# The first norm of a two-block kernel: x in four loads, the bias transposes moved behind the first units, and one matmul for the second half's sum

## The reference, cut to what matters

```python
def rmsnorm(x, g):
    xf = x.astype(jnp.float32)
    y = xf * lax.rsqrt(jnp.mean(xf * xf, axis=-1, keepdims=True) + EPS)
    return (y * g.astype(jnp.float32)).astype(x.dtype)

# first_block
h = rmsnorm(x, norm_mix[l])
proj = h @ w_in[l]
zu, zv, zq, zf, zi, zo, g_a, g_b = jnp.split(proj, split_points, axis=-1)
...
# second_block: the only use of the bias b_ada
mod = (c_act @ w_ada[l] + b_ada[l]).reshape(b, N_MOD, 1, D_MODEL)
```

## Time and profile before

| what | us |
|---|---|
| median of 3 runs | 2746.13 (2746.02 to 2748.16) |
| the profiled execution | 2748.0 |
| its span in the profile | 2745.8 |
| mean granted TensorE clock | 0.997 |
| PE busy | 2710.0 |
| DVE busy | 1425.8 |
| ACT busy | 926.3 |
| POOL busy | 69.2 |

### The profile page before, as it was taken

The page is one execution under the profiler, slowest core; times in us unless marked ns, Lnnn a source line. Parts: engine busy times, 40 slices in busy tenths (PEclk is TensorE's granted clock), DMA queues, the critical chain, the costliest instruction groups (busy, mean ns, idle before and its releaser), DMA issues.

```text
span 2745.8 us, 32619 instructions
## 1 busy us (share of the span) xinstructions
PE 2710.0 (99%) x13015; PEld 2264.0 (82%) x13015; DVE 1425.8 (52%) x1590; ACT 926.3 (34%) x1153; POOL 69.2 (3%) x119
## 2 busy tenths in 40 slices
PE   8999999999999999999989999999999999999999
PEld 7888988888888788888768888888888888888887
DVE  6677563586667675657445323353333454533333
ACT  4555442332223322224444222243222332432221
POOL 1000000000000000001200000000000000000000
PEclk9999999999999999999999999999999999999999
DMA  4111223555664455654112332223323323233322
GB/s 140 58 63 63 69 87 105 179 199 197 208 210 162 156 198 198 218 189 127 47 46 92 103 97 92 89 94 101 99 92 98 101 84 101 85 99 101 98 92 77
DMA packets 257851, 323.67 MB, mean 118 GB/s; under 512 B 5734, under 2 KB 248676, under 8 KB 249572
## 3 DMA queue, kind: packets, MB, share of 16 engines
q1 hardware_dynamic: 245872, 245.12, 28.0%
q0 software_dynamic: 9216, 75.50, 7.4%
q10 hardware_dynamic: 2676, 1.84, 0.2%
HBM read 320.34 MB, written 2.10 MB: 117 GB/s over the span
## 4 chain that ended last, share of the span: by engine, by line
PE 96%; DVE 2%; ACT 1%; issue 0%; DMA 0%; DVEq 0%; ACTq 0%
PE po L682 25%; PE po L683 25%; PE po L684 25%; PE pm L905 2%; PE po L867 1%; PE po L869 1%; PE po L868 1%; PE po L747 1%; PE po L749 1%; PE po L762 1%; PE po L782 1%; PE po L787 1%; PE po L777 1%; PE po L859 1%; PE po L861 1%; PE po L860 1%
## 5 line engine op out<-in xcount | busy, mean ns | idle before, releaser
L1925 DVE TENSOR_TENSOR w_lo<-w_raw,w_hi 128x1024 fp32r<-128x1024 f32 x472 | 562.7, 1222 | 448.3 <-ACT w_hi L1334 445.9
L1334 ACT ACTIVATE w_hi<-w_raw 128x1024 fp32r<-128x1024 f32 x470 | 477.1, 1051 | 886.9 <-PE po L684 869.2
L682 PE MATMUL po<-a_hi,w_hi 128*128 128x512 f32 x1856 | 722.8, 389 | 0.0
L684 PE MATMUL po<-a_hi,w_lo 128*128 128x512 f32 x1856 | 722.1, 389 | 0.0
L683 PE MATMUL po<-a_lo,w_hi 128*128 128x512 f32 x1856 | 722.0, 389 | 0.0
L684 PEld LDWEIGHTS po<-a_hi,w_lo 128*128 128x128 f32 x1856 | 348.3, 188 | 72.8
L682 PEld LDWEIGHTS po<-a_hi,w_hi 128*128 128x128 f32 x1856 | 348.4, 188 | 72.6 <-issue 0.2
L683 PEld LDWEIGHTS po<-a_lo,w_hi 128*128 128x128 f32 x1856 | 348.4, 188 | 71.9 <-issue 0.2
L682 PE MATMUL po<-b_hi,w_hi 128*128 128x512 f32 x1024 | 399.0, 390 | 0.0
L684 PE MATMUL po<-b_hi,w_lo 128*128 128x512 f32 x1024 | 398.4, 389 | 0.0
L683 PE MATMUL po<-b_lo,w_hi 128*128 128x512 f32 x1024 | 398.3, 389 | 0.0
(11 more groups left out here) (380 smaller groups left out, 2862.5 us busy)
## 6 DMA issues: line engine op xcount, KB each, us to landing
ada_in<-in_w_ada_dram POOLq DMA_DIRECT2D x64, 1152.0 KB, 5.5
w_raw<-in_ffn_wg_dram SPq DMA_DIRECT2D x44, 1024.0 KB, 5.3
w_raw<-in_ffn_wu_dram SPq DMA_DIRECT2D x44, 1024.0 KB, 5.3
w_raw<-in_w_ff_dram SPq DMA_DIRECT2D x32, 1024.0 KB, 5.4
w_raw<-in_ffn_wd_dram SPq DMA_DIRECT2D x32, 1024.0 KB, 5.0
w_raw<-in_w_in_dram SPq DMA_DIRECT2D x27, 1024.0 KB, 5.1
w_raw<-in_ffn_wd_dram SPq DMA_DIRECT2D x16, 768.0 KB, 4.3
w_raw<-in_w_in_c_dram SPq DMA_DIRECT2D x12, 1024.0 KB, 5.1
```

What stands on the lines that cost most here:

```text
L682: pe.matmul(o, wh, hi[:, k, :], start=(k == ks[0]), stop=False)
L684: mm = pe.matmul(o, wl, hi[:, k, :], start=False, stop=(k == ks[-1]))
L1334: act.activation(w_hi[:, s, part], w_raw[:, s, part], ACT.Copy).then_inc(hi_done, 1)
L1925: dve.tensor_tensor(w_lo[:, s, part], w_raw[:, s, part], w_hi[:, s, part].bitcast(F32), ALU.subtract).then_inc(lo_done, 1)
```

## The change

Four things are done.

- x comes in four loads of 128 tokens each, with a semaphore each. `turn(j, h, t)` transposes one token block of a quad, two transposes, and PE waits for each load and then transposes its part of all four quads; the quad is announced with the second of its blocks. Quad 3 of half b is now transposed and copied with the others, before the vectors, and DVE's copy of it no longer stands between t1 and t2.
- ACT's square of quad 2 of half b stands before the log of half a, instead of behind its root.
- For half b POOL adds the two sums once more (`quad`), and then the two 256-column halves of the result (`fold`), and PE needs one matmul, `sum_of_second`, instead of four.
- The two bias transposes move on PE from before the first half's sum to behind `first_products`.

```diff
-            for h in range(2):
-                sp.dma_start(x_in[:, 2 * h:2 * h + 2, :],
-                             x[0, 2 * h * P:2 * (h + 1) * P, :].rearrange("(t p) d -> p t d", p=P))\
-                    .then_inc(x_landed[h], 16)
+            for t in range(NT):
+                sp.dma_start(x_in[:, t, :], x[0, t * P:(t + 1) * P, :]).then_inc(x_landed[t], 16)
...
+            pool.wait_ge(s_pre_pool, pre_pool.after("add2b"))
+            pool.tensor_tensor(sq_mix[:, 1, 0, :], sq_mix[:, 1, 0, :], sq_mix[:, 1, 2, :], ALU.add)\
+                .then_inc(s_pre_pool, pre_pool.one("quad"))
+            pool.wait_ge(s_pre_pool, pre_pool.after("quad"))
+            pool.tensor_tensor(sq_mix[:, 1, 0, H[0]], sq_mix[:, 1, 0, H[0]], sq_mix[:, 1, 0, H[1]], ALU.add)\
+                .then_inc(s_pre_pool, pre_pool.one("fold"))
...
-            def turn(j, h):
+            def turn(j, h, t):
                 dst = pm[:, j, :] if h == 0 else po[:, j // 2, j % 2, :]
                 for b in range(2):
-                    for t in range(2):
-                        mm = pe.transpose(dst[:, (2 * b + t) * P:(2 * b + t + 1) * P],
-                                          x_in[:, 2 * h + t, (2 * j + b) * P:(2 * j + b + 1) * P], ident[:, :])
-                mm.then_inc(s_pre_pe, pre_pe.one(f"x{j}{'ab'[h]}"))
+                    mm = pe.transpose(dst[:, (2 * b + t) * P:(2 * b + t + 1) * P],
+                                      x_in[:, 2 * h + t, (2 * j + b) * P:(2 * j + b + 1) * P], ident[:, :])
+                if t:
+                    mm.then_inc(s_pre_pe, pre_pe.one(f"x{j}{'ab'[h]}"))
...
+            def sum_of_second():
+                pe.wait_ge(s_pre_pool, pre_pool.after("fold"))
+                pe.matmul(pm[:, 1, H[1]], ones[:, :], sq_mix[:, 1, 0, H[0]], start=True, stop=True)\
+                    .then_inc(s_n_pe, norm_pe["mix"].one("sumb"))
+
+            for h in range(2):
+                for t in range(2):
+                    pe.wait_ge(x_landed[2 * h + t], 16)
+                    for j in range(QUADS):
+                        turn(j, h, t)
             pe.wait_ge(vec_landed, 12 * 16)
             pe.wait_ge(s_pre_dve, pre_dve.after("x2a"))
             pe.transpose(pm[:, 2, 0:112], vec_rows[0:112, :], ident[0:112, 0:112])\
                 .then_inc(s_pre_pe, pre_pe.one("vec"))
-            turn(QUADS - 1, 1)
-            pe.wait_ge(s_pre_dve, pre_dve.after("x3a"))
-            for l in range(2):
-                if l == 1:
-                    pe.wait_ge(s_pre_dve, pre_dve.after("vec"))
-                pe.transpose(pm[:, 3 - l, 0:MODS], b_rows[:, l, :], ident[0:MODS, 0:MODS])\
-                    .then_inc(s_pre_pe, pre_pe.one(f"b{l}"))
-            first_sum_of(0)
+            sum_of_first()
...
             first_products(U_HG, "mix")
+            for l in range(2):
+                pe.transpose(pm[:, 3 - l, 0:MODS], b_rows[:, l, :], ident[0:MODS, 0:MODS])\
+                    .then_inc(s_pre_pe, pre_pe.one(f"b{l}"))
             product(0, U_HG + 2, DK, a_hi, a_lo)
...
                 first_weight_hi(0)
+                square(2, "b")
                 log("a")
                 root("a")
-                square(2, "b")
                 square(3, "b")
...
                 t(0, "a")
                 t(1, "a")
-                turned(QUADS - 1, "b")
                 t(2, "a")
```

More of the change, by code:

```diff
@@ L244, in hybrid_two_block_kernel @@
         out_taken = [sem("out_taken0"), sem("out_taken1")]
-        x_landed = [sem("x_landed0"), sem("x_landed1")]
+        x_landed = [sem(f"x_landed{t}") for t in range(NT)]
         first_landed = sem("first_landed")
@@ L271, in hybrid_two_block_kernel @@
         s_o_pe, s_o_dve, s_o_act = sem("out_pe"), sem("out_dve"), sem("out_act")
[L274 to L278, removed]
+        pre_pe = Steps(s_pre_pe, [f"x{j}{half}" for half in "ab" for j in range(QUADS)] + ["vec", "b0", "b1"])
+        pre_dve = Steps(s_pre_dve, ["zero"] + [f"x{j}{half}" for half in "ab" for j in range(QUADS)]
+                        + ["vec", "b0", "b1", "c1", "c2", "c3"])
+        pre_pool = Steps(s_pre_pool, ["add0a", "add2a", "add0b", "add2b", "quad", "fold"])
         pre_act = Steps(s_pre_act, ["ec"])
@@ L290, in hybrid_two_block_kernel @@
             if name == "mix":
-                names = ["sq0a", "sq1a", "sq2a", "sq3a", "sq0b", "sq1b", "lna", "rstda", "sq2b", "sq3b"]
+                names = ["sq0a", "sq1a", "sq2a", "sq3a", "sq0b", "sq1b", "sq2b", "lna", "rstda", "sq3b"]
                 names += ["hi0a", "hi1a", "hi2a", "hi3a", "lnb", "hi4a", "rstdb", "hi5a", "hi6a", "hi7a"]
@@ L750, in first_products @@
                         if half == "a" and k == 2 and name == "mix":
-                            first_sum_of(1)
+                            sum_of_second()
                         elif half == "a" and k == 2:
@@ L811, in _, with sum_of_first @@
             pe.wait_ge(consts_ready, 15)
-            def turn(j, h):
+            def turn(j, h, t):
                 dst = pm[:, j, :] if h == 0 else po[:, j // 2, j % 2, :]
                 for b in range(2):
-                    for t in range(2):
-                        mm = pe.transpose(dst[:, (2 * b + t) * P:(2 * b + t + 1) * P],
-                                          x_in[:, 2 * h + t, (2 * j + b) * P:(2 * j + b + 1) * P], ident[:, :])
-                mm.then_inc(s_pre_pe, pre_pe.one(f"x{j}{'ab'[h]}"))
-            def first_sum_of(h):
+                    mm = pe.transpose(dst[:, (2 * b + t) * P:(2 * b + t + 1) * P],
+                                      x_in[:, 2 * h + t, (2 * j + b) * P:(2 * j + b + 1) * P], ident[:, :])
+                if t:
+                    mm.then_inc(s_pre_pe, pre_pe.one(f"x{j}{'ab'[h]}"))
+            def sum_of_first():
                 for j in (0, 2):
-                    pe.wait_ge(s_pre_pool, pre_pool.after(f"add{j}{'ab'[h]}"))
+                    pe.wait_ge(s_pre_pool, pre_pool.after(f"add{j}a"))
                     for b in range(2):
-                        mm = pe.matmul(pm[:, h, H[h]], ones[:, :], sq_mix[:, h, j, H[b]],
+                        mm = pe.matmul(pm[:, 0, H[0]], ones[:, :], sq_mix[:, 0, j, H[b]],
                                        start=(j == 0 and b == 0), stop=(j == 2 and b == 1))
[L827 to L834, removed]
+                mm.then_inc(s_n_pe, norm_pe["mix"].one("suma"))
+            def sum_of_second():
[7 more added lines that the diff above has]
+                        turn(j, h, t)
             pe.wait_ge(vec_landed, 12 * 16)
@@ L2071, in t @@
                                              ALU.mult, ALU.mult).then_inc(nd.sem, nd.one(f"t{k}{half}"))
[L2073 to L2076, removed]
+                for half in "ab":
+                    for j in range(QUADS):
+                        turned(j, half)
                 dve.wait_ge(s_pre_pe, pre_pe.after("vec"))
@@ L2088, in first_norm @@
                 for k in range(4, DK):
-                    if k == DK - 2:
-                        dve.wait_ge(s_pre_dve, pre_dve.after(f"x{QUADS - 1}b"))
                     t(k, "a")
```

## The result

| | before | changed kernel |
|---|---|---|
| median, us | 2746.23 (13 runs) | 2754.05 (13 runs) |
| lowest to highest | 2746.02 to 2748.45 | 2751.34 to 2754.87 |
| span of the profiled execution | 2745.8 | 2751.9 |

The ratio of the means is 1.0025, with a 95% interval of 1.0018 to 1.0032: the changed kernel is slower. Forecast was 2753.2, between 2749.3 and 2756.3.

The account below looks back on a forecast made before the run. TensorE, busy 99% of the span, was taken to bound the kernel. The terms -2.8 (front) + 7.4 (stall) + 2.5 (clock) gave +7.1: 2755.1 for the profiled execution, 2753.2 on the median, range 2749.3 to 2756.3.

Parts of the forecast that it names:

- The stall: TensorE's third unit waits for DVE's queue behind the moved bias transposes, starting at T + 7.4 (bounds 7.1 to 7.7).
- The clock behind it: After the wait before the third unit, TensorE runs 5 us at half clock: 2.5 lost, between 1.7 and 3.4.
- The front: Start of the kernel up to the first products: 3.8 - 1.0 = 2.8 us gained, from 1.2 to 5.4.
- POOL's chain: POOL's third and fourth steps behind half b's last square: end at 18.9 undisturbed, sum put at 20.1 with delay.
- a delay of POOL by DVE: POOL's adds for half b held by DVE's scalings and weight split: 1.2 us added, from 0 to 2.2.
- the 0.7 of the estimate: POOL's last add for half b, over half the columns: about 0.7 us.
- The clock in the front: Granted clock falls before the first product, so products run some 2 us at half clock: 1.0 lost (0 to 2).
- the larger front: Rival: TensorE stays at 2.4 GHz and POOL is not held; front gains 5.4, time 2750.6; chance 0.22.
- Behind that: From the third unit on, nothing gives the lost time back and nothing adds.
- the queue is not hidden: Answers the rival that unit 2's low half is ready when TensorE arrives: 2743.6, or 2741.0 with larger front; chance 0.06.
- x does come early: Answers the rival that the first two x loads land together at 8.9: front -0.1, sum +10.0, 2756.1; chance 0.10.

## Why the prediction was right

The time fell within the range, 0.9 above the forecast, and for the reason given. That the number came so close is in part luck. For the profiled execution the forecast said 2755.1, and it took 2754.05: the terms of the sum came to +6.1 and not +7.1. Then 1.9 was taken off, as if the changed kernel's profiled execution lay above its median as the one before did, and it did not. The two errors nearly cancel. Step by step:

- **The stall** was put at 7.4 and was 7.29, and 7.30 in two more kernels. It was a sum of rows of the kernel before for work that the change leaves as it is; only the instant of its release was new. That is why it was the best of the terms.
- **The clock behind it**: 2.5 expected, 2.07 measured. The low stretch was 4.1 instead of 5; in the run of the move alone it was 5.1 and cost 2.5. The run with the filled stall shows that the mechanism is this.
- **The front** was put at 2.8 and gave 4.07; this is the term that was mis-sized. Most of it is POOL's chain: I let the sum start at 20.1, it started at 18.73. Of these 1.4, 0.6 lie ahead of POOL: the last square ended at 14.8 and not at 15.4, since the log started at 13.33 and not at 13.85. The other 0.8 are a delay of POOL by DVE that was put at 1.2 and came to 0.4. The two did stop each other, but the one that paid was mostly DVE. The earlier trace rows had shown no more than that: there DVE's step was prolonged, and the POOL add beside it, 1.04 like the other three of its shape, was not. Rows of POOL, then DVE, in the changed kernel:

```profile
14.85 1.55 POOL L600 TENSOR_TENSOR sq_mix<-sq_mix 128x512 f32<-128x512 f32 x1 [1.54 <-ACT sq_mix L1460]
16.48 1.34 POOL L603 TENSOR_TENSOR sq_mix<-sq_mix 128x512 f32<-128x512 f32 x1
17.89 0.79 POOL L606 TENSOR_TENSOR sq_mix<-sq_mix 128x256 f32<-128x256 f32 x1
```

```profile
15.17 2.92 DVE L2073 SCALAR_TENSOR_TENSOR ev<-xT,cols,stats 128x256 f32<-128x256 f32 x2
18.02 1.75 DVE L1928 TENSOR_TENSOR w_lo<-w_raw,w_hi 128x1024 fp32r<-128x1024 f32 x1
19.69 0.87 DVE L2073 SCALAR_TENSOR_TENSOR ev<-xT,cols,stats 128x256 f32<-128x256 f32 x2
```

  POOL's three adds took 3.68 in all, where undisturbed ones would be near 3.3 (1.28 + 1.28 + the 0.7 of the estimate): 0.4 of delay, not 1.2. The two scalings beside them took 2.92 instead of the 0.87 of the next two, and 1.91 where POOL had one add only (the run with four matmuls). So DVE lost about 1 us to each of POOL's adds. Of this TensorE felt little: it waited 0.20 for a scaled row at 17.18 and 0.33 for the fold at 18.73. And about 1 us of the 4.07, going by the run of the move alone, comes from the bias transposes no longer standing ahead of the first sum, which the prediction named and gave no price.
- **The clock in the front**: it fell, as expected in the forecast. Put at 1.0, it took 0.8 here (the log came 4.87 earlier, the low rows 4.07), and 1.0 lies between this profile and the one in which it did not fall. For the runs show that it need not: the profile of the kernel with the transposes in the pause kept it. The rival of the larger front is thus a part of the executions, not a thing apart.
- **Behind that**: nothing gave time back, 5.29 at 62 us and 5.30 at 504 us. That nothing is added was wrong by 0.8, in the attention stage, where the low clock fell on other work.
- **The rivals**: the queue is not hidden, and x does come early. The first two loads were not held together: TensorE began at 4.71 where 4.5 was estimated, with the first copy at 7.11 (6.9 forecast). Landing took 3.8 to 7.0 us from issue for the four, so 512 KB loads did as well as the 1 MB loads here.
- **Slips without effect**: the idle stretch ahead of the first product is 3.68 in the earlier trace rows, not 3.66, and the stated range is 0.2 to 0.3 wider at both ends than the bounds worked out for it.

What remains of the change, once the transposes stand in the pause, is 2.8 us of gain (2743.47 against 2746.22), less than the front's own 4 to 5 us in the profiles. The profile of that kernel and the one of before are 5.6 apart (spans 2740.2 and 2745.8), 5.1 of it already at the first `ada_in` load (493.98 against 499.08). The difference to 2.8 is that of profiled execution and median: the profiled one of before is 1.8 above its median, this one 1.1 below. What makes the slower executions of each kernel was not settled; the low clock in the front and the low stretches far behind both come and go from one profile to the next and are of that size.

## What to carry to other kernels

Moving an instruction off a critical path moves also whoever waits for it: look up the consumer in its own engine's order, and count everything that is queued behind it there until something the bounding engine needs. A transfer or a transpose of no urgency is best placed in a pause of its engine that the profile already shows, or its consumer behind the urgent work; either made +8 us into -2 or -3 here. And an idle stretch of the bounding engine can cost, beside its length, what the engine runs at half clock afterwards, here 2 us on 7. A last point: before setting a profile against medians, look up where its execution lies among the others; here that alone is 1 to 2 us, as much as most of the single edits are worth.

## What the runs showed of the hardware

- Two DVE scalings of 256 columns, 0.87 together when alone, took 1.91 beside one POOL add and 2.92 beside two, so each add of 1.28 cost DVE about 1.0. The same adds took 1.55 and 1.34, so they lost 0.3 and 0.1. Where one POOL add and the start of the fold fell on DVE's split of a weight half, both sides lost: the split took 2.30, against 1.21 where POOL was idle (the run with four matmuls), and the fold 1.58 instead of 0.79. The Trainium skill, SBUF — State Buffer, section SBUF: two separate sides, calls it an exclusive lock in which the first holds it for its whole instruction; these numbers agree.
- With the same order of work in front of it and the same idle of 2.16 us, TensorE's granted clock stayed 1.00 in two profiles and went to 0.50 in two others.
- Eight unread matmuls, 7.08 us in a stall of 7.30, kept the granted clock at 1.00 and took the unit behind from 12.95 to 11.05.
- 512 KB loads of x landed 3.8 to 7.0 us after issue, one behind the other, at no visible loss against two of 1 MB (5.2 and 7.7).
